# Two hybrid layers on one core: loads at the start, routing, the first gather and the last expert in another order

## What is computed

```python
mod = silu(cond) @ w_mod + b_mod                     # per group of tokens: sh1, sc1, g1, sh2, sc2, g2
h = rmsnorm(x, norm1_g) * (1 + sc1) + sh1
q, k, v, u, ..., gates = split(h @ w_in)             # 1792 columns, then 3 x 1024 gate columns
x = x + g1 * ((sum over 3 branches of sigmoid(gate_b) * (branch_b @ w_b_o)) @ w_out)
h2 = rmsnorm(x, norm2_g) * (1 + sc2) + sh2
aff = softmax(h2 @ w_router + b_router)              # 16 experts
vals, idx = top_k(aff per expert, n * 2 // 16)       # 64 latent tokens, 16 context tokens
hh = silu(h2[idx] @ w_gate) * (h2[idx] @ w_up)
x = x + g2 * scatter_add(idx, (hh @ w_down) * vals)  # per expert, 12.6 MB of weights
```

## Time and profile before

| | |
|---|---|
| time, median of 3 runs | 2548.26 us (2548.24 to 2552.01) |
| time of the profiled execution | 2548.74 us |
| its span | 2546.9 us |
| mean granted TensorE clock | 0.958 of full |
| busy: TensorE, DVE, ACT, POOL | 90%, 64%, 47%, 11% |
| moved by DMA | 566.10 MB, mean 222 GB/s |

### The profile page before, as it was taken

One profiled execution on the slowest core, in us unless ns is written; L12 is line 12 of the kernel. 1 busy time (PEld: TensorE's weight loads), 2 busy tenths in 40 slices (PEclk: granted clock), 3 DMA queues, 4 the chain that ended last, 5 costly groups with the idle time before them and its releaser, 6 DMA issues.

```text
span 2546.9 us, 37561 instructions
## 1 busy us (share of the span) xinstructions
PE 2301.7 (90%) x14585; PEld 1765.2 (69%) x14585; DVE 1641.2 (64%) x1927; ACT 1205.8 (47%) x1348; POOL 283.7 (11%) x246
## 2 busy tenths in 40 slices
PE   3998899999769999999959988999995999999997
PEld 1777779899546666666647777898994666666664
DVE  1345545534768889888942465454355888988885
ACT  3223323312257777777732232233122677777773
POOL 1012000001121111110011020000012101111101
PEclk8999999999879999999969999999996999999998
DMA  9351110105589999999944410111154999999995
GB/s 333 133 172 63 53 59 34 59 34 182 206 301 365 374 373 373 373 379 375 366 148 166 168 67 20 59 34 59 53 198 167 337 372 373 373 374 376 378 377 184
DMA packets 271390, 566.10 MB, mean 222 GB/s; under 512 B 10568, under 2 KB 12680, under 8 KB 271216
## 3 DMA queue, kind: packets, MB, share of 16 engines
q1 hardware_dynamic: 254848, 509.64, 55.5%
q0 software_dynamic: 14512, 48.05, 6.4%
q10 hardware_dynamic: 1904, 6.62, 0.7%
HBM read 542.71 MB, written 24.18 MB: 223 GB/s over the span
## 4 chain that ended last, share of the span: by engine, by line
PE 83%; DVE 5%; DMA 4%; issue 4%; ACT 3%; DVEq 0%; POOL 0%; SPq 0%; ACTq 0%; POOLq 0%
PE ps L1069 39%; PE ps L770 26%; PE ps L918 6%; PE ps L852 3%; PE ps L894 2%; DMA ring<-in_w_down 2%; PE ps L877 1%; PE ps L710 1%; PE ps L724 1%; DMA ring<-in_w_mod 1%; PE ps L1059 1%; PE ps L988 1%; DVE w_lo L1794 1%; DMA ring<-in_w_in 1%; ACT w_hi L1378 1%
## 5 line engine op out<-in xcount | busy, mean ns | idle before, releaser
L1794 DVE TENSOR_TENSOR w_lo<-ring,w_hi 128x2048 fp32r<-128x2048 f32 x378 | 864.6, 2288 | 134.9 <-ACT w_hi L1378 134.1
L1378 ACT ACTIVATE w_hi<-ring 128x2048 fp32r<-128x2048 f32 x384 | 736.7, 1920 | 315.8 <-PE ps L1069 257.8
L1069 PE MATMUL ps<-w_hi,xT 128*80 128x512 f32 x2048 | 649.1, 396 | 2.2 <-DVE xT L1800 2.2
L770 PE MATMUL ps<-WH,HTH 128*128 128x256 f32 x1840 | 540.3, 294 | 14.7 <-ACT Y L1304 9.0
L770 PE MATMUL ps<-ringL,HTH 128*128 128x256 f32 x1840 | 520.1, 283 | 0.0
L770 PE MATMUL ps<-WH,HTL 128*128 128x256 f32 x1840 | 519.6, 282 | 0.0
L1069 PEld LDWEIGHTS ps<-w_hi,xT 128*80 128x80 f32 x2048 | 306.0, 149 | 173.1 <-issue 4.6
L1069 PE MATMUL ps<-w_lo,xT 128*80 128x512 f32 x1024 | 406.0, 397 | 0.0
L770 PEld LDWEIGHTS ps<-WH,HTH 128*128 128x128 f32 x1840 | 351.6, 191 | 42.2 <-issue 23.1
L770 PEld LDWEIGHTS ps<-ringL,HTH 128*128 128x128 f32 x1840 | 351.9, 191 | 0.8
L770 PEld LDWEIGHTS ps<-WH,HTL 128*128 128x128 f32 x1840 | 351.0, 191 | 0.0
(11 more groups left out here) (198 smaller groups left out, 2145.0 us busy)
## 6 DMA issues: line engine op xcount, KB each, us to landing
ring<-in_w_gate SPq DMA_DIRECT2D x128, 1024.0 KB, 11.3
ring<-in_w_up SPq DMA_DIRECT2D x128, 1024.0 KB, 10.2
ring<-in_w_down SPq DMA_DIRECT2D x128, 1024.0 KB, 11.8
ring<-in_w_mod SPq DMA_DIRECT2D x23, 2048.0 KB, 8.1
ring<-in_w_in SPq DMA_DIRECT2D x18, 2048.0 KB, 7.9
ring<-in_w_out SPq DMA_DIRECT2D x4, 2048.0 KB, 10.6
ring<-in_w_o SPq DMA_DIRECT2D x4, 1536.0 KB, 6.4
Y<-x_save POOLq DMA_DIRECT2D x10, 512.0 KB, 7.4
```

What stands on the lines that cost most here:

```text
L770: last = nc.tensor.matmul(dst, a[:, t, k], w, start=k == 0 and i == 0, stop=k == KB - 1 and i == 2)
L1069: last = nc.tensor.matmul(ps[0:CE, bank], lhs[:, a, kb], w[:, u, k], start=kb == 0 and i == 0, stop=kb == KB - 1 and i == 2)
L1378: nc.scalar.activation(w_hi[:, u % UB], ring[:, raw[0], 4 * (u % 2):4 * (u % 2) + 4], ACT.Copy).then_inc(hi_ready, 1)
L1794: TT(w_lo[:, u % UB], ring[:, raw[0], 4 * (u % 2):4 * (u % 2) + 4], w_hi[:, u % UB].bitcast(f32), ALU.subtract).then_inc(lo_ready, 1)
```

## The change

1. *First loads.* ScalarE issues the loads of x and of the rotary table only when the second conditioning chunk has arrived. POOL issues its tables when the last tile of x has arrived; the copy of x to `x_save` moves behind `store_row(5)`. The slots of the three ring chunks rotate by one. ScalarE makes the norms between the third and the fourth conditioning copy; the splits of the first two weight units move behind the first two tiles (DVE's behind the first low part).
2. *Conditioning columns.* `first_row` goes; four products of 2 columns (`first_cols`) make the columns from the copied partial sums, which have two buffers.
3. *Tiles and groups.* Only two tiles are turned ahead of the projection groups; each of the other three ahead of one of the first three groups. This holds in both layers.
4. *Routing.* `h2_tile` and `route` come one tile earlier; `h2` of a tile directly behind its mean. Of the next layer's conditioning products one stands among the routes, ahead of the first half of the last but one, and three behind the affinities' transposes. Chunks `next` 2 and 3 trade places and slots.
5. *First gather.* POOL makes no low parts. DVE makes those of units 0 and 1 behind the indices, unit 2 behind the first gathered rows. DVE's wait for the gate rows (`g2_ready`) moves behind its first step.
6. *Last expert.* Its `hh` is turned between the two halves of the down product ahead of it, and its parts go into xT.

```diff
+NEXT = [(("next", 0), 0), (("next", 1), 1), (("next", 3), 2), (("next", 2), 0)]
+PRE = [([(("first", c), (c + 1) % 3) for c in range(3)] if l == 0 else []) + MIXER + (NEXT if l + 1 < DEPTH else [])
...
 @@ POOL
+                if l == 0:
+                    pool.wait_ge(x_in[NT - 1], 16)
                 raw(wsraw, A["b_ws"][l].rearrange("g p q -> p g q"))
...
-                if l == 0:
-                    pool.dma_start(xs_d[0:512], A["x_sample"][0]).then_inc(x_saved, 16)
-                    pool.dma_start(xs_d[512:640], A["x_prompt"][0]).then_inc(x_saved, 16)
                 store_row(0)
...
                 for i in range(3, 6):
                     store_row(i)
+                if l == 0:
+                    pool.dma_start(xs_d[0:512], A["x_sample"][0]).then_inc(x_saved, 16)
+                    pool.dma_start(xs_d[512:640], A["x_prompt"][0]).then_inc(x_saved, 16)
                 save_kv(0)
...
-                for u in range(AHEAD):
-                    pool.wait_ge(hi_ready, l * UNITS_E + u + 1)
-                    pool.tensor_tensor(w_lo[:, u % UB], ..., ALU.subtract).then_inc(lo_ready, 1)
...
 @@ TensorE
                 def first_cols(at, c):
+                    pe.wait_ge(part1_ready, at * MOD1 + c + 1)
                     for i in range(4):
                         n = 2 * (4 * c + i)
-                        last = nc.tensor.transpose(ps[:, 0, n:n + 2], modrow1[:, 128 * i:128 * i + 128], ident[0:2, 0:2])
+                        last = nc.tensor.matmul(ps[:, 0, n:n + 2], modpart1[c % 2][:, 128 * i:128 * i + 128], fold[:, 0:2], ...)
...
+                h_tile(0)
+                h_tile(1)
...
                     if u == 0:
                         pe.wait_ge(ht_lo, l * NT + t + 1)
+                        if t + 2 < NT:
+                            h_tile(t + 2)
...
-                    if t >= 2:
-                        h2_tile(t - 2)
-                        if t >= 3:
-                            route(t - 3)
+                    if t >= 1:
+                        h2_tile(t - 1)
+                        if t >= 2:
+                            route(t - 2)
                 ahead = l + 1 < DEPTH
                 if ahead:
                     first_group(l + 1, 0)
-                h2_tile(NT - 2)
-                route(NT - 3)
-                if ahead:
-                    first_group(l + 1, 1)
+                route(NT - 2, range(KB // 2))
                 h2_tile(NT - 1)
-                route(NT - 2)
+                route(NT - 2, range(KB // 2, KB))
                 route(NT - 1).then_inc(rt_done, 1)
...
+                    if b and last_pair:
+                        down(e, n + 8, 0)
+                        turn_hidden(e, 2)
+                        down(e, n + 8, 1)
...
 @@ ScalarE
+            arrived(act, 0, ("first", 1))
             for t in range(NS):
                 act.dma_start(x[:, t], A["x_sample"][0, 128 * t:128 * t + 128]).then_inc(x_in[t], 16)
...
+                    for c in range(MOD1):
+                        if c == MOD1 - 1:
+                            norms()
                         first_part(0, c)
...
+                for u in range(2):
+                    hi(u, u, raw_of(0, 0, True, u))
                 parts(xT, 0)
+                hi(2, 2, raw_of(0, 0, True, 2))
...
 @@ DVE
                         if w == WU - 1:
                             if t:
-                                h2(t - 1)
+                                h2_out(t - 1)
                             mean(1, t)
-                            if t >= 2:
-                                h2_out(t - 2)
+                            h2(t)
...
+                for u in range(2):
+                    lo(u, u, raw_of(0, 0, True, u))
                 parts(xT, 0)
+                lo(2, 2, raw_of(0, 0, True, 2))
                 step(0, 0, True, False)
+                dve.wait_ge(g2_ready, l * 32 + 32)
```

More of the change, by code:

```diff
@@ L659, in _ @@
                 pool.sem_inc(moe_init, 2)
-                settle(pool, 2)
-                for u in range(AHEAD):
-                    pool.wait_ge(hi_ready, l * UNITS_E + u + 1)
-                    slot = raw_of(0, 0, True, u)[0]
-                    pool.tensor_tensor(w_lo[:, u % UB], ring[:, slot, 4 * (u % 2):4 * (u % 2) + 4],
-                                       w_hi[:, u % UB].bitcast(f32), ALU.subtract).then_inc(lo_ready, 1)
-                for u in range(AHEAD):
-                    pool.wait_ge(lo_ready, l * UNITS_E + u + 2)
                 pool.wait_ge(idx_ready, l + 1)
@@ L982, in h2_tile, with route @@
                     turn_tile(H_2, t, cols(xn[:, t % 2]))
-                def route(t):
+                def route(t, part=range(KB)):
                     for h in range(2):
                         pe.wait_ge(hq_free[h], l * (HQ // 2) + 2 * NT + t + 2)
-                    for k in range(KB):
+                    for k in part:
                         last = nc.tensor.matmul(ps[:, 6, E * t:E * t + E], HT[:, t, k], wr[:, k],
@@ L1088, in step, with turn_hidden, down @@
                         turn_rows(j + b, 1 - b, 2 * e + 1, 4 * e + 2)
[L1089 to L1090 removed]
+                    if b and last_pair:
+                        down(e, n + 8, 0)
+                        turn_hidden(e, 2)
+                        down(e, n + 8, 1)
+                    else:
+                        if not start:
+                            for h in range(2):
+                                down(e, n + 8, h)
+                        turn_hidden(e, 3)
+                def turn_hidden(e, freed):
                     for h in range(2):
                         pe.wait_ge(hh_ready, l * 32 + (2 * e + h + 1))
[L1093 removed]
+                        pe.wait_ge(mq_free[h], l * 32 + (2 * e + freed))
                         turn_part([hh[0:CE, 512 * h + 128 * i:512 * h + 128 * i + 128] for i in range(4)], 4 + h)
[L1096 to L1102 removed]
+                def down(e, n, h):
+                    if h == 0:
+                        for b in range(2):
+                            pe.wait_ge(mq_free[b], l * 32 + (2 * e + 2))
+                    pe.wait_ge(out_evac[h], l * E + (e - 1))
+                    chunk(n + 2 * h, 2 * h, hT, 6 + h)
                 pe.wait_ge(moe_init, l * 2 + 2)
@@ L1190, in _ @@
                 if l == 0:
-                    first_part(0, 0)
-                    for c in range(1, MOD1):
+                    for c in range(MOD1):
+                        if c == MOD1 - 1:
+                            norms()
                         first_part(0, c)
-                        first_row(0, c - 1)
-                    first_row(0, MOD1 - 1)
                     first_cols(0)
-                split(0)
-                split(1)
-                if l:
+                else:
+                    split(0)
+                    split(1)
                     norms()
@@ L1214, in _ @@
                     nc.scalar.activation(HTH[:, t].rearrange("p k n -> p (k n)"), hm[:, t % 2], ACT.Copy).then_inc(ht_hi, 1)
+                    if l == 0 and t < 2:
+                        split(t)
                 def mod_part(i):
@@ L1403, in step @@
                             parts(xT, 4 * e + 2)
+                        if s == 10 and b and last_pair:
+                            parts(xT, 4 * e + 2)
                 act.wait_ge(moe_init, l * 2 + 2)
@@ L1520, in _ @@
                         h_lo(t - 2)
+                    if l == 0 and t == 2:
+                        split(0)
                 h_out(NT - 1)
```

88 lines of the change are left out of this document (23 added, 65 removed).

## The result

The changed kernel took 2519.05 us (median of 4 runs, 2511.03 to 2526.23), the kernel before 2548.25 beside it (2544.97 to 2552.01): a ratio of 0.9881, 95% interval 0.9864 to 0.9898. It is 29 us faster, where 43 were forecast; 2505.5 was said, with a range of 2497 to 2517. The time lies 2 us outside that range. A second measurement gave 2517.3 against 2547.4, ratio 0.988 (0.9863 to 0.9898). The profiled execution took 2517.75 us with a span of 2515.9, against 2548.74 and 2546.9: a gain of 31.0 us.

A forecast was written before the change was run, and what follows sets the result against it. TensorE, 83% of the chain, was taken as the bound, so only its pauses and slow-clock stretches could gain. Terms 14.6 − 4 + 2.7 + 12.7 + 11 + 2.5 + 3.5 = 43 us gave 2505.5 us, range 2497 to 2517.

The forecast's parts named there:

- start: Start of the kernel: first conditioning chunks travel alone, gain columns ready at 42 instead of 56.7 us; 14.6 us gained.
- copy of x moved: At layer 0's first gate chunk: the copy to x_save collides with its load and TensorE idles; 4 us lost, bounds 0 to 7.
- routing, layer 0: End of layer 0's routing: a turn and route move into the output groups, one conditioning product leaves the path; 2.7 us gained.
- index copies: Layer 0, behind routing: three DVE copies no longer slowed by POOL's subtractions, 13.2 us becomes 0.5; 12.7 us gained.
- first gather, layers 0 and 1: Before the expert products: DVE's low parts, 4.6 us, lie beside a gather of 7 us and are covered; 0 lost.
- last expert: End of both expert phases: no pause for hT and no fallen clock; 5.8 and 5.1 us gained, together 11.
- start and routing, layer 1: Layer 1: group 0 starts earlier with turns interleaved, 2.5 us; less routing work after the last group, 3.5 us gained.
- Rival (1): Layer 0's experts: weight supply binds, late units cost what TensorE gained beyond it; price 9.6 us, 2515; chance 0.10.
- (3): Start: no gain, x lands behind the conditioning chunks and norms run to 48 us; price 8 to 10, 2514; chance 0.09.
- (4): Layer 0's index copies: DVE stays slow because of the DMA, so the edit fails there; 2518 us; chance 0.04.
- (2): At the gate chunk: the collision with the copy of x doesn't happen or is covered; 2501.5 us; chance 0.12.
- (5): Expert phases, both layers: supply loses its lead early and TensorE's clock falls at each pause; slower, 2570 us; chance 0.03.

The follow-up runs named there:

- e7: Changed kernel with x's and rope's loads issued first again by ScalarE and GpSimd's loads not held; 2525.5 us, ratio 0.992 to the kernel before.
- e1: Changed kernel with only the copy of x to x_save moved behind the second save of keys and values; 2511.2 us, ratio 0.9861 to the kernel before.
- e2: Changed kernel with the copy of x to x_save back at its old place ahead of row store 0; 2511.5 us, ratio 0.9869 to the kernel before.
- e6: Changed kernel with the last update, second norm, its turns and the router products in their old order; 2519.6 us.
- e10: Changed kernel with the first three low parts made on GpSimd again in both layers; 2527.0 us.
- e9: Changed kernel with the last expert in its old order in both layers, hT in one buffer; 2533.6 us.

## Why the prediction was wrong

| step | forecast | in the profile | by its own experiment |
|---|---|---|---|
| start | 14.6 | 17.4 | loads' order 8.5 to 10.6 (e7) |
| copy of x moved | −4 | −10.2 | −8.2 to −11.0 (nine profiles against e1 and e2) |
| routing, layer 0 | 2.7 | 0.0 (mix) | reorder −1.4 to −2.3, product moved +3.0 (e6); 0.9 in all by the stretch around the update |
| index copies | 12.7 | 12.7 | 12.9 (e10) |
| first gather, layers 0 and 1 | 0 | −1.2, −3.7 | −1.9, −3.9 (e10) |
| last expert | 5.8 + 5.1 | 6.6 + 5.3 | 6.8 + 4.1 (e9) |
| start and routing, layer 1 | 2.5 + 3.5 | 4.2 (pre) | start 2.1 by its own stretch, no run of its own; reorder 0.7 to 1.2 (e6), 1.9 in the profile |
| sum | 43 | 31.1 | |

Three steps failed: the copy by 6.2 us, the gather by 4.9, the routing with the start of layer 1 by 4.5. The start and the last expert gave 3.8 more than said, which leaves 12 of the 43 missing. The 4.5 are read from mix and pre, which spread by more than that. By the stretches around the update the routing is short by 1.8 us in layer 0 and by 1.6 in layer 1. The start of layer 1 held: the 216th projection product ends 69.7 us behind the last expert product of layer 0 in the kernel before and 67.6 in the changed one, 2.1 of the 2.5 us said.

"So 1.2 MB takes 7 us or more in place of 3.1: a loss of 4 us" is the largest. The collision was foreseen, and its price was taken wrongly from the start: as a factor of 2.3 on what is left of the chunk. But it isn't a factor. In the start too the weight queue nearly stood still for 7 us while the copy's packets ran (0.17 MB from 24 to 31), and the 12.4 us there are 5.4 for the chunk and 7.0 for the copy. When the copy's packets began at the gate chunk, at 173.3 us, some 1.2 MB of it had moved and about 0.9 were left, less than the 1.2 MB of the prediction. They were still held until the copy was through, and the split came 7.9 us later than it does alone. So in both cases the term is the copy's own duration, 7 to 8 us, though only a part of the load was left. The bound of 7 us was passed by the wait itself (8.4 us in place of 0.5), and the work at the lower clock behind it came on top. The prediction left out that clock; at the gate chunk it had put all of the loss down as TensorE's idle time.

"4.6 us beside a gather of 7" counted VectorE's low parts as hidden by the gather, and didn't ask what they do to it. The low part that runs when the gather is issued holds up the issue, and by finishing early the low parts release a load that passes the gather: 3.9 us in layer 1 and 1.9 in layer 0 (e10).

"Gain 2.7" and "3.5" for the routing took what leaves the tail and only part of what enters the loop. The prediction had put 2.6 us for the turn and route moved into the loop; the loop grew by 3.8, in both layers (2.9 of work and 0.9 of idle time in layer 0). VectorE now makes h2(t) right behind mean(t) and waits for ScalarE's square and root: these waits sum to 6.3 us over the five tiles, where e6 has 1.3 for the squares and none worth a line for the roots. That these waits make the 0.9 us of TensorE's idle time is likely and not shown.

```profile
DVE st L1461 <- ACT EP L1123: 3.3, 5, 1.3
DVE rs L1694 <- ACT rs L1127: 3.0, 5, 1.4
```

The rest held. The columns came at 42.4 (said: 42) and the copies at 0.17. From the last route to the first expert product it was 35.7 us (said: 34 to 35), and the last expert had no pause. Rival (1) is out, since exp fell by the last expert's gain and lost nothing to the supply, although layer 0's experts began 18.7 us earlier. (3) is out by the columns at 42.4, (4) by the copies at 0.17 beside the same loads. (2) went the wrong way: the collision was larger, not absent. The slower case, (5), had no pause to start from. The time of 2519 is near what (3) and (4) gave, and neither was its cause. The chance of faster was right; the range ended 2 us short, because its high side held one missed term at a time, and three came together. Two slips in the working changed nothing: the high bounds add up to 56 and not to 58, and the pause of layer 1's last expert, put at 3.5 us, is 3.2.

## What to carry over

When a transfer moves, place its packets against the nearest load that an engine will wait for. Where two transfers were already seen together, ask whether the wait there was a factor on the load or the other transfer's whole duration: here it was the latter, and a load of which about 0.9 MB was left waited for all of the copy. When work leaves an engine, look at what its new owner does to its neighbour in that very moment: here one subtraction held up a gather's issue and released a load in front of it, and one wait put both right. Work moved ahead of the last dependency gained nothing where its engine was full: in layer 0 it cost 1.4 us.

## What was not expected of the hardware

- A copy of 2.6 MB within HBM, issued by GpSimd, brought SyncE's weight loads nearly to a stop: 0.22 and 0.17 MB in 7 us, where they move 1.11 MB in 3 us alone. Its packets are up to 65 KB, the loads' 2 KB, and about as many of each went through.
- GpSimd's issue of a gather that starts while VectorE subtracts two SBUF tiles ends 0.76 to 0.86 us behind the end of that subtraction (401 of 401), and takes 1.6 to 2.9 us. One that starts within 0.04 us of the subtraction's start, or ahead of it, takes 0.96 to 0.98 (6 of 6), about as without any (0.89 to 0.99).
- A VectorE copy or cast of 16 or 64 columns, from SBUF to SBUF, beside a GpSimd subtraction ends with it: 4.2 to 4.6 us instead of 0.17 to 0.19, six times in two kernels, whichever stood there. MAX8, FIND_INDEX8, MATCH_REPLACE8 and copies out of PSUM keep their time beside such subtractions.
- A gather of 80 rows reached its first turn 2.9 to 3.3 us behind the end of its issue with the engines free, 5.6 to 6.1 with a 2 MB load issued 0.8 us before that end, and 5.5 to 7.3 in layer 0, with several loads in flight.
- Pauses of nearly the same length did not cost the same: behind 3.2 to 3.6 us in the last expert, 48 products took 13.6 to 13.8 us in layer 0, and in layer 1 12.8 in the kernel before and 11.2 in e9.
- Identical executions differ by up to 15 us (2511 to 2526) in the changed kernel and 17.5 in e9, with half-clock stretches of TensorE at different places. What starts one was not settled.
